# Input projection of a hybrid decoder step on one core: block 0 alone and first, the other blocks in pieces beside the expert gathers

## Chip, cores and metric

One NeuronCore of one Trainium2 chip. The metric is the device time of one execution of the whole program in microseconds (us). All data is float32.

## What is computed

The reference takes 1024 prompt tokens (8 blocks of 128) and 8 sample tokens through one layer of width 1024:

```python
qr, kr, vr, gr, qs, ks, vs = project_in(rms_norm(x, norm1_g), w_in, pos)   # w_in: 1024 x 2816
o_ret, state = retention(qr, kr, vr)          # 4 heads of 128, a state carried from block to block
o_swa = sliding_window_attention(qs, ks, vs)  # 8 query heads, 2 key heads of 64, window 128, sinks
h = x + concat(norm(o_ret) * silu(gr), o_swa) @ w_out
x2 = rms_norm(h, norm2_g)
s = (x2 @ peer_w_q) . sub_keys                # 16 score rows of 128 for each token
idx, gates = two-stage top 16 of each of 8 heads          # 128 experts for each token
y = rms_norm(h + sum_k gelu(peer_u[idx_k] . x2) * gates_k * peer_v[idx_k], final_g)
```

Each token reads 128 rows of the table `peer_uv` (16384 rows of 2048 floats, 8 KB each). Outputs also are the retention state and the key and value windows of prompt and samples. The sample tokens use a given state (2 MB) and given caches of 127 + 1 keys and values.

## The kernel before

**Stages.** First everything is projected, then a loop runs over the 8 blocks.

1. Start-up (`token_transposes`, `project_first`, `key_weights`, the loop over `c` at L528). The 9 token tiles (8 blocks, one tile of 8 sample rows) are normalised, transposed and kept. Eight chunks of `w_in` (352 columns, 1.4 MB) arrive in two buffers; with each, block 0 and the sample rows are projected, and between them `key_weights` multiplies `peer_w_q` by the sub keys (16 steps of two halves) into `keyw`.
2. The rest of the projection (`project_rest`, 56 tiles: 8 chunks of `w_in`, loaded a second time, by 7 blocks). ScalarE copies each tile to a staging buffer (`rest_out`), SyncE stores it to `proj_scratch` (L372). The weights and transposed tokens of this stage lie in `ring`, the home of the gathered rows. Between the tiles the kernel runs the sample rows' attention (`sample`, steps 1 to 8, after tiles 2 to 16) and block 0's `front`: `mixing` (rotation, retention, sliding window) and `picking` (output projection L687, norm, scores L704, the top 16 on VectorE from L1282 on).
3. The expert loop over blocks `b`. GpSimd issues one indirect DMA for each of 128 slots (L452): it brings one 8 KB row for each of 128 tokens (1 MB) into one of 8 rows of `ring`. VectorE makes the dot product (L1431), ScalarE the gelu and a scaled diagonal (`weigh`, L972), TensorE adds the pair of rows to `acc` (`add_pair`, L727) and signals `used`, which lets GpSimd fetch into the rows again. So at most 8 gathers are under way.

**Order of the work.** Every engine runs its own list in order. In the expert loop each engine calls `advance(steps, due, tick)` after each slot: a generator yields the tick (0 to 127, one for each slot) from which its next step of block b+1's `front` may run. The ticks are written by hand: `mixing` at 8 to 41, `picking` from `PICK_AT` = 43, the two halves of the top 16 from `PICK_AT + TOPK_AT` = 77, `HALF_TICKS` = 25 apart. A step that is due waits for its semaphores, and everything behind it on that engine waits too. SyncE issues all plain DMAs in one queue, each behind its wait. The first gather waits for block 0's first half of choices; rows 3 to 7 of the ring and all of TensorE's pairs wait until the last of the 56 tiles is done (L464, L759).

**Homes.** `wo` (32 KB of each partition) holds the sub keys, then the sample rows' caches and state, and only then `w_out`, loaded once (L388). `ring` has 64 KB of each partition.

Of the kernel before, what the change touches and what calls it, by code (L numbers as in the profile page):

```python
# [7 lines left out]
F32 = mybir.dt.float32  # L8
# [38 lines left out]
FIRST = 2 * NCH  # L47
REST = (NB - 1) * NCH
# [10 lines left out]
def step_at(table, tiles):  # L59

    return next((step for step, at in table.items() if at == tiles), 0)


class Steps:


    def __init__(self, eng, sem):
        self.eng, self.sem, self.n, self.base = eng, sem, 0, 0
# [5 lines left out]
    def sync(self):  # L74

        self.eng.wait_ge(self.sem, self.base + self.n)

    def enter(self, turn, per):
        self.first, self.per = self.n, per
        self.base = turn * per  # L80

    def leave(self, turns):
        assert self.n - self.first == self.per, (self.n - self.first, self.per)
        self.base, self.n = 0, self.first + turns * self.per

# [4 lines left out]
def early(q):  # L90

    return 8 + (q - 16) * 11 // 4
# [15 lines left out]
def build(nc, A, out):  # L108
    ctx = ExitStack()
    with ctx:  # L110
# [36 lines left out]

        def heads_of(j):

            return (F[2], F[3]) if j == 0 else (F[1], F[4])  # L150
# [27 lines left out]
        o1 = [0]  # L178

        def part(n):  # L180
            o1[0] += n
            return ring[:, o1[0] - n:o1[0]]

        projs = part(D_IN)
        ropes = part(256)
        sT = part(96)
        ss = part(64)
        sr = part(P)
        pts = part(64)
        osT = part(32)  # L190
        wbuf = [part(KC * CW).rearrange("p (k n) -> p k n", k=KC)]
        early_rows = o1[0] // ROWW
        wbuf.append(part(KC * CW).rearrange("p (k n) -> p k n", k=KC))
        xTrest = part(KC * (NB - 1) * P).rearrange("p (k t) -> p k t", k=KC)
        swp = [h, proj]
        xa = [h[:, :], xlo[:, :]]
        wqT = [work[:, 0:D], work[:, D:2 * D]]
        staging = [(xlo, gfb)[i // 2][:, i % 2 * CW:(i % 2 + 1) * CW] for i in range(STG)]
        mask0 = xlo[:, 2 * CW:2 * CW + 2 * P]


        wof = wo[:].rearrange("p k n -> p (k n)")
        skT = wof[:, 0:NSC]
        xTfirst = wof[:, NSC:NSC + KC * (P + NS)].rearrange("p (k t) -> p k t", k=KC)
        kw = wof[:, 0:NS * P].rearrange("p (s c) -> p s c", s=NS)
        vw = wof[:, D:D + NS * P].rearrange("p (s c) -> p s c", s=NS)
        kwT, sel8 = wof[:, 2 * D:3 * D], wof[:, 3 * D:4 * D]
        st_s = wof[:, 4 * D:8 * D].rearrange("p (s h e) -> p s h e", s=NS, h=RH)

        def token_rows(n):  # L210

            return NS if n == 1 else P

        def tokens_T(n, k):

            if n < 2:
                return xTfirst[:, k, n * P:n * P + token_rows(n)]
            return xTrest[:, k, (n - 2) * P:(n - 1) * P]
# [3 lines left out]
        ld_wq = [sem("ld_wq0"), sem("ld_wq1")]  # L222
        ld_x = [sem("ld_x0"), sem("ld_x1")]
        ld_w = [sem("ld_w0"), sem("ld_w1")]
        ld_wo, ld_gf = sem("ld_wo"), sem("ld_gf")
# [7 lines left out]
        ld_proj, ld_res, ld_mask0 = sem("ld_proj"), sem("ld_res"), sem("ld_mask0")  # L233
# [22 lines left out]
            "rowsx", "roped", "columns", "silu_out", "kv")}  # L256

        proj_d = nc.dram_tensor("proj_scratch", [NTOK, D_IN], F32).ap()
        w_in_v = A["w_in"].rearrange("(k p) n -> p k n", p=P)
# [4 lines left out]
        N_CONST = 8 + NS  # L264
# [8 lines left out]
        def _(sp):  # L273
            def load_x(n):

                if n >= 2:
                    sp.wait_ge(xn_T, n - 1)
                src = x_s if n == 1 else x_p[max(n - 1, 0) * P:max(n, 1) * P, :]
                sp.dma_start(xa[n % 2][0:token_rows(n), :], src).then_inc(ld_x[n % 2], 16)

            def load_w(n):

                if n >= 2:

                    sp.wait_ge(pj_mm, 2 * (n - 1) if n - 2 < NCH else FIRST + (NB - 1) * (n - 1 - NCH))
                c = n % NCH
                sp.dma_start(wbuf[n % 2], w_in_v[:, :, c * CW:(c + 1) * CW]).then_inc(ld_w[n % 2], 16)

            def load_wqT(n):

                if n >= 2:
                    sp.wait_ge(keyw_mm, 2 * n - 2)
                sp.dma_start(wqT[n % 2], A["wqT"][n]).then_inc(ld_wq[n % 2], 16)

            load_x(0)
            for dst, src in [(ident[:], A["c_ident"]), (fold[:], A["c_fold"]), (g1c, A["norm1_g"].rearrange("(k p) -> p k", p=P))]:
                sp.dma_start(dst, src, allow_slow_non_contiguous=True).then_inc(ld_first, 16)
            load_x(1)
            load_w(0)
            load_x(2)  # L300
            load_w(1)
            load_x(3)
            sp.dma_start(skT, A["sub_keysT"]).then_inc(ld_skT, 16)
            load_wqT(0)
            load_wqT(1)
            for c in range(NCH):
                if c + 4 < TILES:
                    load_x(c + 4)
                if 2 * c + 2 < NHC:
                    load_wqT(2 * c + 2)  # L310
                load_w(c + 2)
                if 2 * c + 3 < NHC:
                    load_wqT(2 * c + 3)


            sp.wait_ge(pj_out, FIRST)
            sp.dma_start(proj_d[SEQ:NTOK, C_KS:D_IN], projs[0:NS, C_KS:D_IN]).then_inc(sm["kv"], 16)
            sp.dma_start(ropes[0:NS, :], A["c_rope"][SEQ:NTOK, :]).then_inc(sm["columns"], 16)

            sp.wait_ge(pj_mm, FIRST)  # L320
            sp.wait_ge(keyw_mm, 2 * NHC)
            for s in range(NS):
                sp.dma_start(kw[0:P - 1, s, :], A["cache_swa_k"][s, 1:P].rearrange("w k d -> w (k d)")  # L323
                             ).then_inc(sm["kw"], 16)
            sp.dma_start(st_s.rearrange("p s h e -> p (s h) e"),
                         A["state_ret"].rearrange("s h d e -> d (s h) e")).then_inc(sm["kw"], 16)
            sp.wait_ge(sm["kv"], 16)
            sp.dma_start(kw[P - 1:P, :, :], proj_d[SEQ:NTOK, C_KS:C_VS].rearrange("(a s) c -> a s c", a=1)
                         ).then_inc(sm["kw"], 16)
            for s in range(NS):  # L330
                sp.dma_start(vw[0:P - 1, s, :], A["cache_swa_v"][s, 1:P].rearrange("w k d -> w (k d)")  # L331
                             ).then_inc(sm["vw"], 16)
            sp.dma_start(vw[P - 1:P, :, :], proj_d[SEQ:NTOK, C_VS:D_IN].rearrange("(a s) c -> a s c", a=1)
                         ).then_inc(sm["vw"], 16)
            sp.dma_start(sel8[0:NS, :], A["c_sel8"]).then_inc(sm["vw"], 16)

            sp.wait_ge(xn_T, TILES)
# [7 lines left out]
            for dst, src in loads:  # L345
                sp.dma_start(dst, src, allow_slow_non_contiguous=True).then_inc(ld_const, 16)
# [1253 lines left out]
```

## Time and profile before

| | |
|---|---|
| three runs, us | 3264.59, 3268.72, 3270.58 (median 3268.72) |
| the profiled execution, its own time and its span | 3263.53 us and 3261.7 us |
| busy | TensorE 2315.3 us (71%), VectorE 2024.6 us (62%), ScalarE 1021.3 us (31%), GpSimd 1191.9 us (37%) |
| read from and written to memory | 1143.51 MB and 17.87 MB |
| mean granted TensorE clock | 0.841 |

How to read it: the span runs from the first to the last instruction of the profiled execution; 1.8 us lie around it. Busy times are unions of an engine's instructions. A DMA share is the mean busy share of the core's 16 DMA engines. A clock of 1.00 is 2.4 GHz, 0.50 is 1.2 GHz. A float32 matmul appears as two records, so eight matmuls are "x16".

### The profile page before, as it was taken

The numbers are of one execution on the slowest core, as the hardware profiler recorded it, in microseconds if no ns is written. First come the engines' busy times: TensorE is split into PE (matmuls) and PEld (weight loads), VectorE is DVE, ScalarE is ACT, GpSimd is POOL, SyncE is SP. The second block draws the span as 40 slices with busy tenths as digits, with TensorE's granted clock in tenths as the row PEclk, the third lists the DMA queues.
The fourth block names the chain that finished last, engine by engine and source line by source line (L and its number), as shares of the span: only waits on it lengthen the run. The fifth ranks groups of instructions, "written<-read, shape, count | busy, mean of one in ns | idle before, by whom it ended". The sixth has DMA issues, their size and how long they took to land.

```text
span 3261.7 us, 29956 instructions
## 1 busy us (share of the span) xinstructions
PE 2315.3 (71%) x7730; PEld 863.8 (26%) x7730; DVE 2024.6 (62%) x4947; ACT 1021.3 (31%) x3222; POOL 1191.9 (37%) x1052
## 2 busy tenths in 40 slices
PE   7989996676567656775677567855785678558654
PEld 5556553321122212221222122211221122111111
DVE  2113035658865786579656875687568766875864
ACT  3211101422343234323432334323432343233221
POOL 0000002444444444444444444443444344444442
PEclk9978998897788877887888788878887689789777
DMA  6334215999999999999999999999999999999996
GB/s 221 132 108 138 69 43 210 421 421 408 415 399 422 408 405 409 413 404 406 414 406 395 415 415 410 392 420 409 402 405 410 415 410 421 389 414 422 408 421 279
DMA packets 199565, 1167.67 MB, mean 358 GB/s; under 512 B 23592, under 2 KB 57664, under 8 KB 66272
## 3 DMA queue, kind: packets, MB, share of 16 engines
q0 software_dynamic: 148608, 1082.20, 81.3%
q1 hardware_dynamic: 50784, 83.85, 7.4%
q14 instruction: 147, 1.20, 0.1%
q8 instruction: 26, 0.43, 0.1%
HBM read 1143.51 MB, written 17.87 MB: 356 GB/s over the span
## 4 chain that ended last, share of the span: by engine, by line
DMA 40%; PE 35%; issue 10%; DVE 7%; ACT 5%; SPq 2%; POOL 2%; POOLq 0%; DVEq 0%; ACTq 0%
DMA ring<-in_peer_uv,idxg 38%; PE ps L727 14%; PE ps L496 10%; PE ps L704 7%; DVE ring L1431 3%; POOL ring L452 2%; ACT ring L803 1%; PE ps L478 1%; PE ps L521 1%; DMA out<-work 1%; DVE proj L1289 1%; ACT small L972 1%; PE ps L687 1%; SPq L323 1%; SPq L331 1%
## 5 line engine op out<-in xcount | busy, mean ns | idle before, releaser
L727 PE MATMUL ps<-ring 128*64 128x512 f32 x4096 | 1307.0, 772 | 861.5 <-ACT ring L803 858.0
L452 POOL DMA_INDIRECT ring<-in_peer_uv,idxg x1024 | 1176.0, 1148 | 1495.8 <-PE ps L727 1235.0
L1431 DVE SCALAR_TENSOR_TENSOR ring<-ring,xlo 128x1024 f32<-128x1024 f32 x512 | 626.5, 1224 | 386.3 <-DMA ring<-in_peer_uv,idxg 324.5
L1431 DVE SCALAR_TENSOR_TENSOR ring<-ring,xhi 128x1024 f32<-128x1024 f32 x512 | 626.5, 1224 | 383.2 <-DMA ring<-in_peer_uv,idxg 372.3
L727 PEld LDWEIGHTS ps<-ring 128*64 128x64 f32 x4096 | 300.0, 164 | 1769.0 <-ACT ring L803 1292.8
L972 ACT ACTIVATE small<-small 128x2 f32<-128x2 f32 x512 | 104.1, 203 | 1710.5 <-DVE ring L1431 1710.0
L803 ACT ACTIVATE ring<-gdiag,small 128x64 f32<-128x64 f32 x1024 | 300.3, 340 | 17.7 <-ACT small L972 1.1
L803 ACT ACTIVATE gdiag<-fold,gateg 128x64 f32<-128x64 f32 x1024 | 292.7, 333 | 1.5
L496 PE MATMUL ps<-ring 128*128 128x352 f32 x896 | 278.2, 470 | 7.3 <-ACT xlo L803 6.5
L704 PE MATMUL ps<-keyw,work 128*128 128x512 f32 (+1 forms) x576 | 265.1, 603 | 0.0
L496 PEld LDWEIGHTS ps<-ring 128*128 128x128 f32 x896 | 172.9, 195 | 107.4 <-issue 14.0
L459 POOL COPY idxg<-stage 128x64 uint32<-128x64 uint32 x16 | 7.1, 445 | 526.9 <-DMA stage<-moving 500.1
L704 PEld LDWEIGHTS ps<-keyw,work 128*128 128x128 f32 (+1 forms) x576 | 98.0, 179 | 165.5 <-issue 164.3
L1296 DVE FIND_INDEX8 proj<-proj 128x8 uint32<-128x128 f32 (+3 forms) x432 | 135.0, 328 | 0.0
L1289 DVE MAX8 proj<-proj 128x8 f32<-128x128 f32 (+3 forms) x432 | 109.5, 321 | 37.1 <-ACT proj L803 36.3
L687 PE MATMUL ps<-wo,work 128*128 128x512 f32 x256 | 123.9, 618 | 0.0
L496 PE MATMUL ps<-ring,wo 128*128 128x352 f32 (+1 forms) x256 | 79.4, 464 | 0.0
L972 ACT ACT_TABLE_LOAD x60 | 77.0, 1283 | 1.1
L687 PEld LDWEIGHTS ps<-wo,work 128*128 128x128 f32 x256 | 46.3, 194 | 79.1 <-issue 78.2
L1304 DVE MATCH_REPLACE8 proj<-proj 128x128 f32<-128x128 f32 (+3 forms) x216 | 66.8, 319 | 0.0
L803 ACT ACTIVATE xlo<-ps 128x352 f32<-128x352 f32 x28 | 12.9, 463 | 170.5 <-PE ps L496 143.7
L1068 DVE RECIPROCAL small<-small 128x1 f32<-128x1 f32 (+3 forms) x36 | 5.9, 164 | 86.2 <-ACT small L810 86.2
(191 smaller groups left out, 1527.3 us busy)
## 6 DMA issues: line engine op xcount, KB each, us to landing
ring<-in_w_in SPq DMA_DIRECT2D x16, 1408.0 KB, 6.3
ring<-in_peer_uv,idxg POOLq DMA_INDIRECT x1024
proj<-proj_scratch SPq DMA_DIRECT2D x7, 1408.0 KB
work<-in_wqT SPq DMA_DIRECT2D x16, 512.0 KB, 5.4
h<-in_x_prompt SPq DMA_DIRECT2D x13, 512.0 KB, 5.0
proj_scratch<-xlo SPq DMA_DIRECT2D x28, 176.0 KB, 1.9
proj_scratch<-gfb SPq DMA_DIRECT2D x28, 176.0 KB, 1.8
wo<-in_w_out SPq DMA_DIRECT2D x1, 4096.0 KB, 13.8
```

The lines of the kernel that those rows point to most:

```text
L323: sp.dma_start(kw[0:P - 1, s, :], A["cache_swa_k"][s, 1:P].rearrange("w k d -> w (k d)")).then_inc(sm["kw"], 16)
L452: nc.gpsimd.indirect_dma_start(row[r], None, A["peer_uv"], bass.IndirectOffsetOnAxis(ap=experts, axis=0)).then_inc(ld_row[r], 16)
L496: mm = nc.tensor.matmul(bank[0:token_rows(n), 0:CW], tokens_T(n, k), buf[:, k, :], start=(k == 0), stop=(k == KC - 1))
L687: mm = nc.tensor.matmul(F[2 + n][0:rows, :], lhsT, wo[:, k, n * 512:(n + 1) * 512], start=(k == 0), stop=(k == KC - 1))
L704: mm = nc.tensor.matmul(F[2 + n][0:rows, :], xT[:, k * P:k * P + rows], keyw[:, k, n * 512:(n + 1) * 512], start=(k == 0), stop=(k == KC - 1))
L727: mm = nc.tensor.matmul(acc[side * HP:(side + 1) * HP, n * 512:(n + 1) * 512], row_u[r][:, 0:HP], row_v[r][:, n * 512:(n + 1) * 512], star ...
L803: return nc.scalar.activation(o, i, ACT.Copy, **kw_)
L972: me.did(nc.scalar.activation(gel[:, r:r + 2], dot[:, r:r + 2], ACT.Gelu))
L1289: me.did(nc.vector.max(v16(j)[:, r8 * 8:r8 * 8 + 8], rowsof(j)))
L1296: me.did(nc.vector.max_index(i16(j)[:, r8 * 8:r8 * 8 + 8], v16(j)[:, r8 * 8:r8 * 8 + 8], rowsof(j)))
L1304: me.did(nc.vector.match_replace(rowsof(j), v16(j)[:, 0:8], rowsof(j), TAKEN))
L1431: ins = stt(row_u[r], row_u[r], 1.0, (xlo, xhi)[unit % 2][:], ALU.mult, ALU.mult, accum_out=dot[:, r:r + 1])
```

## The change

Block 0 alone is projected in the start-up, with 8 chunks of 352 columns. All other tiles are projected later in 128 pieces of 176 columns (`PIECES`): block 1 in 16 pieces between block 0's scores and the first pair (`BEFORE`), blocks 2 and 3 in 32 pieces (`EARLY`) beside the first third of block 0's gathers, blocks 4 to 7 and the sample rows in 80 pieces up to tick 32 of block 2. Each group of pieces loads `w_in` again (48 loads of 0.7 MB). Weights, tokens and staging of the pieces lie in `wo`, so `w_out` is loaded anew for each of the first blocks: once to `ring` for block 0, then four times to `wo` (`load_wo`). The transposed tokens of blocks 4 to 7 go to memory (`xT_scratch`) and come back twice. The key weights move behind the start-up, between block 0's `front` steps. The sample rows' attention runs beside the gathers of block 2 (from tick 56 of it, `SAMPLE_AT`). `picking` starts at tick 45 instead of 43. Psum buffers are renumbered: F[4] and F[5] are the pieces'. GpSimd's waits for the projection go. The hardware loops over the blocks are written out.

```diff
+LCH = 16
+LW = D_IN // LCH
+LATE_TILES = [(1,)] * LCH + [(2, 3)] * LCH + [(4, 5, 6, 7, NB)] * LCH
+PIECES = [(l, l % LCH, n) for l, tiles in enumerate(LATE_TILES) for n in tiles]
...
+def late_tick(q):
+
+    if q < EARLY:
+        return 3 + (q - BEFORE) * 9 // 8
+    if q < HALFWAY:
+        return 67 + (q - EARLY) * 97 // 40
+    return TICKS + 59 + (q - HALFWAY) * 101 // 40
...
+            def load_w(c):
+
+                if c >= 2:
+                    sp.wait_ge(pj_mm, c - 1)
+                sp.dma_start(wbuf[c % 2], w_in_v[:, :, c * CW:(c + 1) * CW]).then_inc(ld_w[c % 2], 16)
...
+            def load_late(l):
+
+                if 2 <= l < 2 * LCH:
+                    sp.wait_ge(pj_mm, NCH + (LAST_OF[l - 3] + 1 if l > 2 else 0))
+                elif l >= 2 * LCH and l % (LCH // 2) >= 2:
+                    sp.wait_ge(pj_mm, NCH + LAST_OF[l - 2] + 1)
...
+            def sample():
+                yield SAMPLE_AT
...
+                for s in range(NS):
+                    sp.dma_start(kw[0:P - 1, s, :], A["cache_swa_k"][s, 1:P].rearrange("w k d -> w (k d)")
+                                 ).then_inc(sm["kw"], 16)
...
+            for c in range(NCH):
+                if c + 2 < NCH:
+                    load_w(c + 2)
+                if c + 2 < TILES:
+                    load_x(c + 2)
...
+            move_tokens(0)
+            for q in range(BEFORE):
+                load_late(q + 3)
+                if q == 3:
                     move_picks(0, 0)
...
+                store_late(q)
...
+            for b in range(NB - 1):
+                shift = FIRST_SHIFT if b == 0 else 0
+                if b:
+                    late(b, 6)
+                    store_y(b - 1)
+                late(b, 40 + shift)
+                if b < 4:
+                    load_wo(b + 1)
+                load_residual(b + 1)
+                late(b, 84 + shift)
+                move_tokens(b + 1)
+                late(b, 104 + shift)
+                move_picks(b + 1, 0)
...
-            pool.wait_ge(sm["vb_used"], NS)
-            pool.wait_ge(pj_mm, FIRST + REST - (NB - 1))
...
-                        if unit == early_rows:
-
-                            hold(pool, pj_mm, FIRST + REST)
-
...
+            token_transposes(0)
+            for c in range(NCH):
+                project_first(c)
+                token_transposes(c + 1)
...
+            for tick in range(TICKS):
+                due = advance(steps, due, tick)
+                key_due = advance(keys, key_due, tick)
+            for q in range(BEFORE):
+                project_late(q)
...
+            root(tok_root[0])
+            tokens_in(0)
+            root(tok_root[1])
+            root(tok_root[0])
+            for c in range(NCH):
+                first_out(c)
+                tokens_in(c + 1)
+                if c + 3 < TILES:
+                    root(tok_root[(c + 3) % 2][0:token_rows(c + 3), :])
...
+SAMPLE_AT = 2 * TICKS + 56
+FIRST_SHIFT = 8
+PICK_AT = 45
```

`project_late(q)` is eight matmuls of 128x176 into F[4] or F[5]; it waits for its weights and for the copy of piece q-2. `late_out(q)` (ScalarE) copies piece q to staging and waits for the store of piece q-4. `project_first(c)` waits for its chunk and for the copies of token tile c.

## Rows read from the trace of the kernel before

**Rows 1.** The page: the gathers' DMA queue, and the chain that ended last

```profile
q0 software_dynamic: 148608, 1082.20, 81.3%
DMA 40%; PE 35%; issue 10%; DVE 7%; ACT 5%; SPq 2%; POOL 2%; POOLq 0%; DVEq 0%; ACTq 0%
```

**Rows 2.** Stretches: us, PE, PEld, DVE, ACT, POOL busy, clock, DMA share, GB/s

```profile
280.00:554.00 274.00, 245.36 (x852) 151.95 (x853) 82.04 (x302) 42.99 (x91) 7.88 (x9) 0.96 0.32 114
554.00:3217.00 2663.00, 1809.60 (x5775) 555.93 (x5773) 1873.36 (x4479) 909.48 (x2956) 1180.17 (x1036) 0.82 1.00 409
```

**Rows 3.** Timeline of GpSimd, the first and the ninth gather: start, us, instruction

```profile
501.87 1.10 POOL L452 DMA_INDIRECT ring<-in_peer_uv,idxg  x1 [1.05 <-issue]
...
557.91 1.48 POOL L452 DMA_INDIRECT ring<-in_peer_uv,idxg  x1 [23.48 <-PE ps L727]
```

**Rows 4.** Timeline of TensorE, the first pairs

```profile
553.77 8.81 PE L727 MATMUL ps<-ring 128*64 128x512 f32 x32 [23.54 <-ACT ring L803]
```

**Rows 5.** Groups by line and shape: count, busy us, mean ns

```profile
L727 PE MATMUL ps<-ring 128*64 128x512 f32 x4096 | 1307.0, 772 | 861.5 <-ACT ring L803 858.0 <-issue 2.2
...
L496 PE MATMUL ps<-ring 128*128 128x352 f32 x896 | 278.2, 470 | 7.3 <-ACT xlo L803 6.5 <-issue 0.7
L704 PE MATMUL ps<-keyw,work 128*128 128x512 f32 x512 | 236.0, 604 | 0.0
...
L687 PE MATMUL ps<-wo,work 128*128 128x512 f32 x256 | 123.9, 618 | 0.0
```

**Rows 6.** Timeline of the start-up: projection, key weights, token copies, a square sum

```profile
18.80 5.89 PE L496 MATMUL ps<-ring,wo 128*128 128x352 f32 x16
...
61.47 2.05 PE L521 MATMUL ps<-wo,work 128*128 128x128 f32 x16
...
65.14 4.90 PE L496 MATMUL ps<-ring,wo 128*128 128x352 f32 x16
...
65.34 2.17 ACT L803 ACTIVATE ring<-ps,small 128x128 f32<-128x128 f32 x8 [1.19 <-PE ps L478]
...
70.41 1.23 DVE L1085 SCALAR_TENSOR_TENSOR g2b<-xlo 128x1024 f32<-128x1024 f32 x1 [1.83 <-DMA xlo<-in_x_prompt]
```

**Rows 7.** DMA issues: count, KB each, median us from issue to landing

```profile
ring<-in_w_in SPq DMA_DIRECT2D x16, 1408.0 KB, 6.3
...
h<-in_x_prompt SPq DMA_DIRECT2D x13, 512.0 KB, 5.0
...
wo<-in_w_out SPq DMA_DIRECT2D x1, 4096.0 KB, 13.8
```

**Rows 8.** Packets, MB, share of 16 engines: 295 to 298 us, 214 to 218, 304 to 308

```profile
q1 hardware_dynamic: 1700, 0.87, 101.8%
...
q1 hardware_dynamic: 1056, 1.46, 102.0%
...
q1 hardware_dynamic: 405, 1.66, 101.0%
```

**Rows 9.** DMA of 148 to 152 us, only loads of cached keys

```profile
q1 hardware_dynamic: 171, 0.09, 7.2%
```

**Rows 10.** DMA of 1214 to 1228 us, gathers beside plain transfers

```profile
q0 software_dynamic: 585, 4.26, 73.4%
q1 hardware_dynamic: 446, 1.61, 28.5%
```

**Rows 11.** Timeline of VectorE: block 0's rotation, first and last of its top 16

```profile
278.10 1.43 DVE L1107 TENSOR_TENSOR proj<-work 128x256 f32<-128x256 f32 x4
...
444.47 1.65 DVE L1289 MAX8 proj<-proj 128x8 f32<-128x128 f32 x8 [36.26 <-ACT proj L803]
...
473.42 0.22 DVE L1361 SCALAR_TENSOR_TENSOR proj<-proj 128x64 f32<-128x64 f32 x1
```

**Rows 12.** A stretch in which TensorE waited: columns as in rows 2

```profile
158.00:172.00 14.00, 0.04 (x1) 0.00 (x0) 0.00 (x0) 0.25 (x1) 0.00 (x0) 0.60 0.56 161
```

More of the change, by code:

```diff
@@ new lines, in _ @@
+            steps, keys = front(0), key_weights()
+            due, key_due = next(steps), key_tick(0)
+            for tick in range(TICKS):
+                due = advance(steps, due, tick)
+                key_due = advance(keys, key_due, tick)
+            for q in range(BEFORE):
+                project_late(q)
+            pe.wait_ge(keyw_out, 2 * NHC + 2)
+            pieces, sample_ = late_pieces(), sample()
+            late_due, sample_due = next(pieces), next(sample_)
+            for b in range(NB):
+                if b:
+                    pe.wait_ge(acc_out, b)
+                add_residual(b)
+                steps = front(b + 1) if b < NB - 1 else picking(NB, NS, LAST_AT)
@@ L991, in sum_out @@
                 copy(xT, acc).then_inc(acc_out, 1)
-            steps = front(0)
-            due = next(steps)
-            for q in range(REST):
-                rest_out(q)
-                sample(step_at(SAMPLE_AT, q + 1))
-                due = advance(steps, due, early(q))
-            due = advance(steps, due, TICKS)
-            begin(0)
-            for p in range(EDGE):
-                weigh(0, p)
-            with act.Fori(0, NB - 1) as b:
-                me.enter(b, ACT_STEPS)
-                roots.enter(b, 3)
-                steps = front(b + 1)
+            act.wait_ge(ld_first, 48)
@@ new lines, in _ @@
+            root(tok_root[0])
[7 more added lines that the diff above has]
+                    root(tok_root[(c + 3) % 2][0:token_rows(c + 3), :])
+            steps, keys = front(0), key_weights()
+            due, key_due = next(steps), key_tick(0)
+            topk = PICK_AT + TOPK_AT
+            for tick in range(topk + HALF_TICKS):
+                due = advance(steps, due, tick)
+                key_due = advance(keys, key_due, tick)
@@ L1007, in _ @@
+            for q in range(BEFORE):
+                late_out(q)
+            steps_0, due_0 = steps, due
+            pieces, sample_ = late_pieces(), sample()
+            late_due, sample_due = next(pieces), next(sample_)
+            for b in range(NB):
+                begin(b)
+                if b:
+                    sum_out(b - 1)
+                steps = front(b + 1) if b < NB - 1 else picking(NB, NS, LAST_AT)
                 due = next(steps)
-                for p in range(EDGE, PAIRS):
+                for p in range(PAIRS):
+                    tick = 2 * p + 1
@@ L1463, in _ @@
+            due = next(steps)
+            topk = PICK_AT + TOPK_AT
+            steps_0, due_0 = steps, advance(steps, due, topk + HALF_TICKS - 1)
+            sample_ = sample()
+            sample_due = next(sample_)
+            for b in range(NB):
+                take_over(b)
+                steps = front(b + 1, wmask[:]) if b < NB - 1 else picking(NB, NS, LAST_AT)
                 due = next(steps)
-                for unit in range(2 * EDGE, SLOTS):
+                for unit in range(SLOTS):
```

1029 lines of the change are left out of this document (517 added, 512 removed).

## The prediction

> **What bounds the kernel now.** I read the stretches first. From 554 us to 3217 us the 16 DMA engines are busy all the time (share 1.00), while TensorE is busy 1810 of 2663 us [rows 2]. Ahead of that, from 280 to 554 us, their share is 0.32. The queue table says who fills them: the gathers take 81.3% of 16 engines' span, 2652 us, and in the chain DMA has the largest share, 40% [rows 1]. So from 554 us on every byte that is added costs its DMA time, and idle TensorE or ScalarE time there is worth nothing. The other bound is the start-up: the first gather is issued at 501.87 us, the ninth at 557.91 us [rows 3], because the pairs begin at 553.77 us [rows 4]. The change trades one against the other. It brings the pairs forward, and it moves transfers from a stretch with idle DMA engines into one without. Two sums decide: when do the pairs begin, and what do the moved and added transfers cost.
>
> **Start-up, block 0 alone.** One would think that eight projections of 4.9 us and a few transposes [rows 6] take 60 us. The queues say otherwise. SyncE issues chunk c+2 and behind it token tile c+2, and the chunk waits for projection c. ScalarE does the root of tile c+2 ahead of the copies of tile c+1, without which projection c+1 can't start. So a period holds, one after the other: chunk and tile landing, 6.3 us and 1.4 us behind it (a tile's 128 packets of 4096 B at 160 ns over 16 engines, and as much again for contention) = 7.7; square sum 1.23 and three short operations, 2.0; the copy of the chunk, 0.5; the token copies 2.17; the projection 4.9 [rows 6 to 8]. That is 17.3 us. The first projection ends at about 18 us (before, it began at 18.80 with the same loads under way [rows 6]), six periods follow, and a last one without a load, 9 us. TensorE works 6 of 17 us; where it waited like that the granted clock was 0.60, so partly 1.2 GHz [rows 12]. At 1.2 GHz the period would be 22 us; I take 19.5. End of projection 7: 18 + 117 + 10 = 145 us, rotation done at 151. Bounds: 131 and 160.
>
> **Block 0's front with the key weights.** Before, it ran from the rotation at 278 us to the top 16 at 444 us [rows 11], 166 us, filled by projection tiles of 278.2/56 = 5.0 us [rows 5]. Now 32 halves of key weights at 1.02 us [rows 6] stand between. Retention and sliding window are a ping-pong of engines, estimated at 42 us with 16 halves in their gaps; then the output projection 123.9/8 = 15.5 us at the mean clock, 13.7 at full clock; norm and transposes beside 8 halves, 14; two score groups of 236.0/32 = 7.4 us, at full clock 6.85, with 8 halves of 1.2 us put between them, 23 [rows 5]; one copy, 1. Sum 94 us, and 5 for a lower clock: the top 16 starts at 250 us. It takes 29.0 us [rows 11] and 1.5 for the end, the move and the first gather 3.8: first gather at 284 us. Bounds of this part: 76 us (TensorE's own work) to 120.
>
> **The sixteen pieces of block 1** stand ahead of the first pair. Seven are done while the top 16 runs; for the others SyncE issues the weights only behind `move_picks`, so they compete with the first 8 gathers. A piece is 4.9/2 = 2.4 us of TensorE. Its weights are 1024 packets, 64 for each engine. In the gather stretch plain packets and gather packets pass about one for one (446 to 585 in 14 us) [rows 10]. So a load lasts up to 64 x (36 + 320) ns = 22.8 us while gathers are queued, and 2.3 us when they have run dry. (320 ns is 2652 us x 16 over some 132,000 rows of 8 KB [rows 1].) I take 23 us for the first, then 7 x 3.5: pairs begin 48 us after the first gather, at **332 us**, 222 us sooner than at 554. Bounds 296 and 357.
>
> **What the gather stretch gets.** Prices by packet from [rows 8]: 512 B 48.9 us / 1700 = 28.7 ns, 1408 B 61.8 ns, 4096 B 159.6 ns; 704 B lies between, 35.8 ns. After the pairs begin:
> - 29 loads of 176 columns (l = 19 to 47): 29 x 1024 x 35.8 / 16 = 66.5 us
> - 96 stores of full tiles: 96 x 128 x 35.8 / 16 = 27.5 us (the samples' 16 are nothing)
> - `w_out` four times: 4 x 1024 x 159.6 / 16 = 40.9 us
> - kept tokens twice, 4.3 MB at 415 GB/s: 10.3 us
> - sample rows: state in 5.1, out 4096 x 28.7 / 16 = 7.3, window stores 3.7 us
> - the 16 loads of cached keys and values. Here I priced by the row, not by bytes: in 4 us 171 packets at 7.2% of 16 engines, so one engine alone at 23.4 ns each [rows 9]. 16 x 127 x 23.4 = 47.5 us on one engine that every gather needs too. Cost 47.5, at least 3 if it were spread.
>
> Sum 209 us; 165 if the last were free. Nothing in the old gather stretch goes away. Writing out the loops takes nothing off either, as the DMA engines had no gap there.
>
> **Waits.** TensorE, ScalarE and SyncE now wait for transfers inside the loop, with `add_pair` and `weigh` queued behind. Eight gathers in flight cover 8 x 2.56 = 20.5 us. (1) Ticks 3 to 38 of block 0: 32 pieces 75 us, 18 pairs at 1307.0/512 = 2.55 [rows 5], 46 us, and mixing about 20 = 141 us of TensorE; DMA 36 x 2.56 + 16 x 2.3 + 9 = 138. Both full; and ScalarE waits for stores that stand behind weight loads. I take 20 us. (2) `w_out` asked for some 8 ticks (21 us) ahead of its use in blocks 1 and 2, landing in 13.8 us alone [rows 7] and 64 x 0.48 = 31 us beside gathers; tokens and weights at tick 67 likewise: mostly covered, 5 us together. (3) The samples' two waits for the one engine, 10 us beyond its work; block 1's columns behind weight loads, 5. Sum **40 us**, bounds 0 and 100. The pieces' 112 x 2.4 = 269 us of TensorE and 112 short ScalarE copies cost nothing else: the gather stretch has 853 us without TensorE work. Without that cover, as in (1), they are the bound. `picking` two ticks later is hidden by the ring. GpSimd issues the same 1024 gathers.
>
> **Sum.** 3263.5 (the profiled execution) - 222 + 209 + 40 = 3290.5 us. The median of the three runs is 5 us above that execution, so **3296 us**, slower by 0.8%.
>
> **Rivals.**
> - *A, faster: the start is early and the waits stay covered.* The gathers' queue would not hold up weight loads. Mechanism: plain packets of 704 B pass several to one gather packet. With 5 at a time a load lasts 2.3 + 13 x 0.32 = 6.5 us, the nine pieces go 17 us sooner, waits (1) and (2) shrink by 25; with the period at 17.3 us, another 19. 3296 - 61 = 3235. For it: the plain packets of [rows 10] have 3.6 KB in the mean, and none of 704 B is shown. It decides from a pair start of about 300 us. The Trainium skill, "DMA: Bandwidth & Descriptors", section "Queues, rings and completion order", says that an engine takes whole packets of typically 9 to 17 descriptors from one queue before it turns to the next; by that rule the load would be as short as here and the sum 3235, by the row it is 3296; the trace does not agree, as the one for one of [rows 10] speaks against it. Chance 0.28.
> - *B, much slower: loads late in the loop become the bound.* A load of 22.8 us has a lead of three weight steps, about 20 us. If each of 29 then stops the pairs by 3 us more than the ring covers, it is 3296 + 29 x 3 = 3383. Against it: when the pairs stop, the gathers run dry and a load takes 2.3 us. Chance 0.15.
> - *C, a draw.* The start-up gain equals the transfers, both by accident: 3268. Chance 0.08.
> - *D, the change does not bring the gathers forward.* If front and keys kept the old 166 us instead of 99, the pairs would start at 399 and the time be 3363. It ends where B does and shares B's chance.
>
> My forecast, slower by 10 to 90 us, has 0.49. The bounds of its terms (-36 and +25 on the start, -44 on the one engine, -40 and +60 on the waits) don't fall together; with A and part of B the range is 3228 to 3365. A measurement here tells 0.2%, 6.5 us, from nothing. Faster 0.28, same 0.08, slower 0.64.
>
> **What would show it.** Right: projection periods of 17 to 22 us in the start-up with ScalarE idle before its roots; first gather near 284 us, pairs near 332; DMA share near 1 from there, with the plain queue's time up by about 209 us; 16 cache loads in block 2 at 22 GB/s or with the pairs stopped; blocks 3 to 7 as before. Wrong: a period near 9 us, weight loads that land in 6 us beside gathers, or DMA gaps of more than 100 us in blocks 0 to 2.

## The result, and the profile after

| | before | after |
|---|---|---|
| median of the runs, us | 3268.44 (3264.59 to 3270.58, 4 runs) | 3322.77 (3316.09 to 3326.58, 4 runs) |
| the profiled execution, its time and its span | 3263.5, 3261.7 | 3324.5, 3322.7 |
| first gather, first pair, us | 501.9, 553.8 | 270.8, 321.9 |
| from the first pair to the end of the span, us | 2707.9 | 3000.8 |

The ratio is 1.0172, 95% interval [1.0159, 1.0184]: the changed kernel is 1.7% slower. The forecast was 3296 us, 0.8% slower; the sign and the range held, but the loss is twice what I said, 54 us and not 27.

The timelines of GpSimd and of TensorE of the changed kernel (start, us, instruction, in brackets the idle time before it and who ended it) show the first, the ninth gather and the first pair, 231 to 233 us sooner than in [rows 3, 4]:

```profile
270.84 1.10 POOL L554 DMA_INDIRECT ring<-in_peer_uv,idxg  x1 [0.97 <-POOL idxg L563]
...
324.56 0.94 POOL L554 DMA_INDIRECT ring<-in_peer_uv,idxg  x1 [43.21 <-PE ps L847]
```

```profile
321.86 3.65 PE L847 MATMUL ps<-ring 128*64 128x512 f32 x16 [1.71 <-ACT ring L918]
```

So the start gained 232 us, and the rest of the program lost 293. The stretches from the first pair on (columns as in rows 2: length, the busy time of five engines, clock, DMA share, GB/s), beside the one of 1.00 in [rows 2]:

```profile
322.00:1000.00 678.00, 528.40 (x2433) 299.26 (x2432) 353.12 (x786) 209.04 (x681) 220.16 (x202) 0.88 0.94 367
1000.00:1800.00 800.00, 535.46 (x2198) 236.91 (x2196) 488.43 (x1191) 248.10 (x789) 284.90 (x256) 0.82 0.91 361
1800.00:3280.00 1480.00, 1005.15 (x3145) 298.46 (x3147) 1061.88 (x2599) 493.49 (x1626) 655.30 (x581) 0.83 1.01 414
```

The last is as full as before. The first two lack 6% of 678 and 9% of 800 us, 113 us of DMA time. The queue table over 322 to 3280 us of the changed kernel (packets, MB, share of 16 engines), and over 554 to 3217 us of the kernel before:

```profile
q0 software_dynamic: 146594, 1067.58, 88.6%
q1 hardware_dynamic: 66911, 80.33, 7.8%
```

```profile
q0 software_dynamic: 146527, 1067.13, 98.1%
q1 hardware_dynamic: 7808, 21.28, 2.2%
```

The plain queue q1 took 7.8% of 2958 us = 231 us, before 2.2% of 2663 = 59: 172 us more. The gathers (q0) took 2621 and 2612, 8 us more. Those two and the gaps, 111 us more by the same rows (100% less the shares: 3.4% of 2958 against -0.4% of 2663), make 291 of the 293 us. The gaps are what is left over, so the sum closes by itself, and each share is rounded to 0.1%, 3 us. The account has three lines: start -232, transfers +180, gaps +111. My forecast had -222, +165 and +85 (44.5 for the one-engine loads, 40 for waits).

Where the gaps are, the waits tell. The view of waits of the changed kernel (engine, line, waited for: us, times, longest), those behind the start-up for transfers other than gathers:

```profile
ACT wo L918 <- DMA proj_scratch<-wo: 100.1, 12, 17.2
DVE work L1216 <- DMA qsT<-in_c_rope: 35.8, 1, 35.8
...
PE ps L578 <- DMA wo<-proj_scratch: 32.1, 1, 32.1
PE ps L805 <- DMA wo<-in_w_out: 31.7, 2, 26.1
DVE work L1216 <- DMA out<-work: 28.8, 4, 20.0
PE ps L686 <- DMA wo<-proj_scratch: 23.9, 1, 23.9
...
PE ps L620 <- DMA wo<-in_w_in: 19.2, 3, 12.5
```

L918 is ScalarE's copy of a piece, which waits until its staging buffer is stored; L1216 the rotation, of block 1 for its columns (35.8 us) and of later blocks until `y` of an earlier block is stored (28.8 us in four waits); L578 and L686 the transposes of the samples' cached keys and the product with their values; L805 `w_out`; L620 the pieces' weights.

The stretches with the large gaps (columns as in rows 2):

```profile
322.00:490.00 168.00, 139.56 (x743) 103.28 (x742) 70.57 (x145) 53.86 (x168) 38.44 (x38) 0.89 0.88 317
580.00:620.00 40.00, 29.37 (x130) 17.72 (x131) 12.74 (x22) 9.57 (x31) 12.27 (x10) 0.82 0.77 294
960.00:1000.00 40.00, 35.98 (x155) 20.61 (x156) 12.33 (x20) 11.19 (x38) 11.88 (x11) 0.88 0.77 296
1195.00:1225.00 30.00, 10.34 (x48) 5.92 (x49) 12.92 (x27) 5.26 (x18) 4.60 (x3) 0.66 0.62 238
1340.00:1540.00 200.00, 103.21 (x404) 36.91 (x402) 106.74 (x292) 49.65 (x156) 56.82 (x54) 0.74 0.79 298
1720.00:1760.00 40.00, 11.35 (x30) 3.76 (x32) 11.10 (x18) 6.33 (x25) 5.84 (x6) 0.66 0.77 311
```

Their gaps are 20 us (the 32 pieces at the start of block 0), 9 and 9 (the first weights of a group), 11 (the rotation that waits for `y`), 42 (the sample rows) and 9 (`w_out` for block 3), 100 of the 113.

### The profile page after: what moved, and what is told of

It reads as the page before. It is cut to its first block, busy times and chain, and to the rows that moved or that the text cites. A ratio compares the mean times of both kernels' runs of the same rounds, so it can differ in the third digit from the quotient of the medians.

```text
span 3322.7 us, 29034 instructions
## 1 busy us (share of the span) xinstructions
PE 2297.2 (69%) x8754; PEld 990.1 (30%) x8754; DVE 2022.9 (61%) x4947; ACT 1028.5 (31%) x3291; POOL 1171.3 (35%) x1052
## 4 chain that ended last, share of the span: by engine, by line
DMA 36%; PE 33%; DVE 11%; issue 6%; SPq 5%; ACT 4%; POOL 3%; another core or an unknown queue 2%; POOLq 0%; DVEq 0%; ACTq 0%
DMA ring<-in_peer_uv,idxg 24%; PE ps L847 13%; PE ps L824 6%; PE ps L620 6%; DVE ring L1538 5%; DMA proj_scratch<-wo 4%; SPq L390 3%; POOL ring L554 3%; DMA wo<-in_w_out 2%; SPq L385 2%; PE ps L601 2%; PE ps L805 2%; ACT ring L918 2%; DMA wo<-in_w_in 2%
## 5 line engine op out<-in xcount | busy, mean ns | idle before, releaser
L554 POOL DMA_INDIRECT ring<-in_peer_uv,idxg x1024 | 1158.0, 1131 | 1834.0 <-PE ps L847 1591.9
L847 PE MATMUL ps<-ring 128*64 128x512 f32 x4096 | 1236.1, 736 | 701.5 <-ACT ring L918 700.8
L847 PEld LDWEIGHTS ps<-ring 128*64 128x64 f32 x4096 | 290.8, 158 | 1490.8 <-ACT ring L918 1016.9
L620 PE MATMUL ps<-wo 128*128 128x176 f32 (+1 forms) x2048 | 351.4, 330 | 87.9 <-issue 68.8
L620 PEld LDWEIGHTS ps<-wo 128*128 128x128 f32 (+1 forms) x2048 | 310.1, 188 | 174.4 <-issue 140.7
L918 ACT ACTIVATE ring<-gdiag,small 128x64 f32<-128x64 f32 x1024 | 300.3, 340 | 16.8
L918 ACT ACTIVATE gdiag<-fold,gateg 128x64 f32<-128x64 f32 x1024 | 292.7, 333 | 1.5
L918 ACT ACTIVATE wo<-ps 128x176 f32<-128x176 f32 (+3 forms) x135 | 41.7, 311 | 449.8 <-PE ps L620 278.7
L805 PE MATMUL ps<-wo,work 128*128 128x512 f32 x224 | 110.9, 629 | 31.7 <-DMA wo<-in_w_out 31.7
L601 PE MATMUL ps<-ring,wo 128*128 128x352 f32 x128 | 56.3, 611 | 69.6 <-ACT ring L918 35.2
L805 PEld LDWEIGHTS ps<-wo,work 128*128 128x128 f32 x224 | 40.2, 195 | 103.9 <-issue 103.9
L1216 DVE TENSOR_TENSOR work<-proj,qsT 128x256 f32<-128x256 f32 x64 | 22.8, 418 | 64.6 <-DMA qsT<-in_c_rope 35.8
## 6 DMA issues: line engine op xcount, KB each, us to landing
wo<-in_w_out SPq DMA_DIRECT2D x4, 4096.0 KB, 33.2
```

Of the source, the lines that this page charges most:

```text
L554: nc.gpsimd.indirect_dma_start(row[r], None, A["peer_uv"], bass.IndirectOffsetOnAxis(ap=experts, axis=0)).then_inc(ld_row[r], 16)
L601: mm = nc.tensor.matmul(F[c % BANKS][:, 0:CW], tokens_T(0, k), wbuf[c % 2][:, k, :], start=(k == 0), stop=(k == KC - 1))
L620: mm = nc.tensor.matmul(F[4 + q % 2][0:token_rows(n), 0:LW], late_T(n, k), buf[:, k, :], start=(k == 0), stop=(k == KC - 1))
L805: mm = nc.tensor.matmul(F[2 + n][0:rows, :], lhsT, weights[:, k, n * 512:(n + 1) * 512], start=(k == 0), stop=(k == KC - 1))
L847: mm = nc.tensor.matmul(acc[side * HP:(side + 1) * HP, n * 512:(n + 1) * 512], row_u[r][:, 0:HP], row_v[r][:, n * 512:(n + 1) * 512], star ...
L918: return nc.scalar.activation(o, i, ACT.Copy, **kw_)
```

## Experiments

Two theories stood against each other for the gaps. **One engine:** the samples' 16 cache loads lie on one DMA engine that all gathers need. **The queue:** SyncE has one plain queue, and what is late in it (stores behind 0.7 MB loads, first weights behind kept tokens) stops ScalarE or TensorE for longer than eight gathers last. Beside them, two prices were to be tested: of the start-up period, and of a load beside gathers. Gains below are differences of the ratios to the kernel before on the same chip, times 3265 us; each ratio has an interval of about ±0.0016, 5 us, so a gain is good to 7 us or so (to 10 where the kernel with three edits is in it). Where stretches or issue times of two kernels are compared, it is one profiled execution of each.

### The cache loads cut in two, after and before

```diff
-sp.dma_start(kw[0:P - 1, s, :], A["cache_swa_k"][s, 1:P]...).then_inc(sm["kw"], 16)
+for lo, hi in ((0, 112), (112, P - 1)):
+    sp.dma_start(kw[lo:hi, s, :], A["cache_swa_k"][s, 1 + lo:1 + hi]...).then_inc(sm["kw"], 16)
```

The same for `vw`; the waits count 2 * NS + 1 transfers.

> The kernel after the change with each of the 16 loads of cached keys and values cut in two, 112 and 15 partitions, so that no load lies on one DMA engine. One-engine theory: what the one engine takes is lost whole, 47.5 us less 3 for the spread work, and the waits of TensorE for the keys (32 us) and of VectorE and TensorE for the values shrink with it: 3268 to 3280 us, 45 to 55 us below the changed kernel, and the stretch of block 2 in which the DMA share fell is full. Rival, the queue of SyncE: the samples' rows wait behind other transfers whatever engine they lie on, and the work would come in 0 to 15 us faster only: 3308 to 3323 us.

Measured: 3275.24 us, ratio 1.0032 [1.0015, 1.0048], against 1.0172: 46 us. The one-engine theory holds. SyncE's timeline and the stretches of the changed kernel show how it stood still:

```profile
1344.53 56.71 SPq L385 DMA_DIRECT2D wo<-in_cache_swa_k  x7
...
1404.27 105.52 SPq L390 DMA_DIRECT2D wo<-in_cache_swa_v  x8
```

```profile
1375.00:1395.00 20.00, 0.41 (x7) 0.32 (x6) 6.04 (x10) 0.25 (x1) 2.50 (x2) 0.60 0.53 204
```

In these 20 us TensorE works 0.4 us, because the transposes of the keys stand in its list ahead of the next pair. In the second half of them the gathers have run dry, and what moves is 22 GB/s, the rate of one engine as in [rows 9]. SyncE too is held: issuing 15 loads takes 162 us. Where nothing else moves it is 3 us each (two in 5.93 us from 1395.31 us), which is one load on one engine (127 packets at 23.4 ns are 2.97 us). With the loads cut, the same stretch of that kernel is full:

```profile
1375.00:1395.00 20.00, 18.24 (x77) 7.73 (x77) 7.87 (x14) 9.46 (x25) 8.34 (x8) 0.99 1.05 375
```

The Trainium skill, "DMA: Bandwidth & Descriptors", section "Why a DMA increments its semaphore by 16 and not by 1", says that a transfer runs on the largest number of engines, up to 16, that divides its outermost dimensions, so that 127 partitions put everything on one. The trace agrees: 22 GB/s with 127, a full stretch with 112 (and 15).

The control does the same in the kernel before:

> The kernel before with the same 16 loads cut into 112 and 15 partitions. There they lie in the start-up beside projections: both theories expect little, 0 to 8 us less than 3268.4. If it gained as much as the changed kernel does, the cut itself and not the place in the loop would be what matters.

Measured: 3240.92 us, ratio 0.9932 [0.9915, 0.9948]: 22 us gained, where I expected 0 to 8. The 16 loads lie in the start-up there, and I had thought them hidden behind projections. They weren't: over 100 to 200 us TensorE is busy 81 us before and 98.6 with the cut. These two lines are of the kernel before and of the one with the cut:

```profile
100.00:200.00 100.00, 81.05 (x365) 54.49 (x363) 5.54 (x14) 16.70 (x34) 0.00 (x0) 0.85 0.33 106
```

```profile
100.00:200.00 100.00, 98.58 (x457) 66.44 (x456) 5.54 (x14) 20.09 (x43) 0.00 (x0) 0.95 0.45 142
```

The first gather comes 27 us sooner with the cut (474.87 and not 501.87 us). So of the 46 us that the loads cost in the changed kernel, 22 were being paid already; moving them into the loop doubled their cost.

### The token tile ahead of the chunk

```diff
 for c in range(NCH):
+    if c + 2 < TILES:
+        load_x(c + 2)
     if c + 2 < NCH:
         load_w(c + 2)
-    if c + 2 < TILES:
-        load_x(c + 2)
```

> The kernel after the change with the token tile c+2 issued ahead of weight chunk c+2 on SyncE, nothing else. Theory (the forecast's account of the period): the tile waits only for the transposes of tile c, so landing, square sum, root and copies run beside the projection, and the period falls from 17 to 19 us to 9 or 10; the first gather and the first pair come about 50 us sooner (from 271 and 322 us to about 220 and 272) and the time falls by as much, to about 3273 us. Rival 1: TensorE's lower clock or the weight chunk itself holds the period (14 us or more): 3300 us or above. Rival 2: the start comes 50 us sooner but the loop gives a part back, as the transfers of blocks 0 to 2 are the same: a gain clearly below the shift of the first pair.

Measured: 3279.76 us, ratio 1.0048 [1.0031, 1.0064]: 40 us, where 50 were expected. A period of the changed kernel, from its timeline:

```profile
68.56 6.60 PE L601 MATMUL ps<-ring,wo 128*128 128x352 f32 x16 [10.66 <-ACT wo L918]
...
75.19 0.40 SPq L327 DMA_DIRECT2D ring<-in_w_in  x1
75.64 0.57 SPq L321 DMA_DIRECT2D xhi<-in_x_prompt  x1
82.44 1.22 DVE L1203 SCALAR_TENSOR_TENSOR keyw<-xhi 128x1024 f32<-128x1024 f32 x1 [15.45 <-DMA xhi<-in_x_prompt]
...
83.89 0.20 ACT L925 ACTIVATE small<-small 128x1 f32<-128x1 f32 x1 [15.47 <-DVE small L1180]
...
84.34 2.16 ACT L918 ACTIVATE ring<-ps,small 128x128 f32<-128x128 f32 x8
86.65 2.10 PE L601 MATMUL ps<-ring,wo 128*128 128x352 f32 x3 [10.62 <-ACT ring L918]
```

It is the ring of the forecast: chunk and tile are issued, the tile lands 6.8 us later, square sum, root, copies, projection. With the tile first, the timeline of that kernel:

```profile
43.81 6.66 PE L601 MATMUL ps<-ring,wo 128*128 128x352 f32 x16 [2.36 <-ACT wo L918]
...
58.05 6.83 PE L601 MATMUL ps<-ring,wo 128*128 128x352 f32 x16 [6.70 <-ACT ring L918]
...
68.11 6.66 PE L601 MATMUL ps<-ring,wo 128*128 128x352 f32 x16 [2.36 <-ACT ring L918]
```

The period is 9.9 to 14.2 us, 11.3 in the mean of seven, where I had expected 9 or 10. The first gather is at 226.9 us, 44 sooner, and the first pair at 275.5, 46 sooner; that arrives in the time, as far as 7 us can be told. One reason for the rest is the projection, which takes 6.7 us and not 4.9 [rows 6]: see the last section.

### The stores on a queue of their own

```diff
+def put_late(q):
+    _, c, n = PIECES[q]
+    act.wait_ge(pj_out, NCH + q + 1)
+    act.dma_start(proj_d[...], late_stage(q)[...]).then_inc(st_pj[q % STG], 16)
 ...
                 yield late_tick(q) + 2
                 late_out(q)
+                yield late_tick(q) + 3
+                put_late(q)
```

SyncE's `store_late` is empty in turn, its waits with it.

> The kernel after the change with the stores of the small pieces issued by ScalarE, on a DMA queue of its own, a tick behind each copy; SyncE no longer waits for the pieces' copies. Queue theory: the 100 us that ScalarE waits for stores which stand behind weight loads, and the waits of SyncE's loads behind stores, make 25 of the excess of idle DMA time: 3298 to 3313 us, ScalarE's wait for the stores under 30 us. Rival: those waits are covered by the eight gathers in flight, and the time stays within 5 us of 3322.8; or ScalarE, which now issues and waits for its own copies, loses a few us (up to 3335).

Measured: 3301.57 us, ratio 1.0121 [1.0104, 1.0138]: 17 us by the ratios, 21 by the medians. ScalarE's wait for stores, 100.1 us, is gone from the waits, and the time lies in the range that the queue theory had (3298 to 3313). But only a part of the gain is what the theory meant. At the end of block 0's 32 pieces the gap shrinks by 6 us (over 440 to 580 us the DMA share is 1.00 where it was 0.96). Another 9 us is the stretch from 1720 to 1760, long behind the last piece: its share is 1.01 and not 0.77, and TensorE's wait of 26 us for `w_out` is gone, because the samples' state, for whose store `w_out` has to wait, was stored in 56 us and not in 81. Why that store was faster here is not shown. SyncE is relieved too: in the changed kernel, beside the first gathers, issuing one store held it for many us:

```profile
272.51 7.15 SPq L351 DMA_DIRECT2D proj_scratch<-wo  x1
...
282.07 13.69 SPq L351 DMA_DIRECT2D proj_scratch<-wo  x1
```

### The first weights of a group asked for earlier

```diff
-        return 67 + (q - EARLY) * 97 // 40
-    return TICKS + 59 + (q - HALFWAY) * 101 // 40
+        return 75 + (q - EARLY) * 87 // 40
+    return TICKS + 67 + (q - HALFWAY) * 91 // 40
 ...
-                    yield late_tick(FIRST_OF[l0]) - 4
+                    yield late_tick(FIRST_OF[l0]) - 12
```

> The kernel after the change with the pieces of blocks 2 to 7 due 8 ticks (about 20 us) later, at tick 75 instead of 67 and packed a little closer, while their first loads are asked for at the same tick as now. Lead theory: TensorE's two waits of 22 us for the first weights (at 590 and 964 us) go, and with them 5 to 10 us of idle DMA each: 3303 to 3313 us. Rival: the eight gathers in flight (20.5 us) cover those waits already and closer packing costs elsewhere: within 5 us of 3322.8.

Measured: 3313.75 us, ratio 1.0153 [1.0136, 1.0170]: 6 us, and the interval reaches that of the changed kernel. Alone it decides nothing. The two gaps close (DMA share 1.02 and 0.98 where it was 0.77), at 590 us, where TensorE waited 22 us,

```profile
590.63 4.32 PE L620 MATMUL ps<-wo 128*128 128x176 f32 x16 [22.37 <-issue]
```

and at 964 us, where it waited 21.6. But the lead is lost again: gather 80 (of 0 to 1023) is issued 16 us sooner than in the changed kernel, gather 112 is 3 us later. The pieces stand closer, and ScalarE waits 127.1 us for stores and not 100.1; that this is the reason is argued and not shown. On top of the other edits this one was worth more (next part).

### All together

> The kernel after the change with three edits together: the loads of cached keys and values cut in two, the token tile issued ahead of the chunk, the pieces' stores on ScalarE's own queue. If the three causes are separate, their gains of 47.5, 43 and 21 us add: 3211 us. If the waits of one hide behind another, less: 3225 to 3240. Both would beat the kernel before.

> As the three edits together, with the later pieces of the lead kernel as well: a further 10 to 20 us, 3191 to 3201 us, if the lead theory holds; the same as the three edits together within 5 us if it does not.

Measured: the three edits 3213.36 us, ratio 0.9856 [0.9830, 0.9881]; with the later pieces 3190.09 us, 0.9776 [0.9760, 0.9792]. Against the changed kernel the three give 3.16% or 103 us, where 46 + 40 + 17 = 103: within the noise, three separate causes that add. The fourth adds 26 us, give or take 10, which is more than the 6 it had alone; against the 10 to 20 that I expected it can't be told apart. With the stores out of the way the lead that it gains at gather 80 is kept (17 us there, 13 at gather 128). The kernel that results is 2.2% faster than the one before the change. Its stretches from the first pair on:

```profile
278.00:950.00 672.00, 545.42 (x2500) 299.14 (x2497) 372.30 (x853) 215.16 (x701) 227.91 (x211) 0.90 0.97 384
950.00:1750.00 800.00, 597.53 (x2336) 254.92 (x2336) 535.14 (x1306) 270.83 (x861) 317.94 (x280) 0.82 0.99 397
```

The gaps are 3% and 1%, 28 us where they were 113. What is left stands mostly at the start of block 0 (share 0.90 over 278 to 446 us) and at the rotation that waits for `y` (0.66 over 1105 to 1140).

### What a load beside gathers costs

Added to the kernel before, in SyncE's loop over blocks, five in each turn; by the trace they were issued beside the gathers of blocks 1 to 6 (891 to 2622 us). In the second kernel without the wait and each copy to its own place:

```diff
+def one_more():
+    if extra[0]:
+        sp.wait_ge(ld_spare, 16 * extra[0])
+    extra[0] += 1
+    sp.dma_start(spare, A["w_in"].rearrange("(k p) n -> p k n", p=P)[:, :, 0:176]).then_inc(ld_spare, 16)
```

> The kernel before, SyncE's loop over blocks written out, with 30 copies of 176 columns of w_in (1024 packets of 704 B each) into a scratch in DRAM spread over blocks 3 to 7 and the gathers beside them; nobody but SyncE waits for one. Price theory: the gather stretch has no gap, so each costs its packets' time, 30 x 1024 x 35.6 ns / 16 = 68 us: 3333 us, give or take 10. Rival: small packets slip in between the gathers' packets and cost less than half of that: under 3300 us. If it comes to clearly more than 80 us, loads cost the loop more than their own time even where no engine waits for them.

> As the kernel before with added copies, of which that run's trace shows 25 (25 x 1024 packets; the 30 in its expectation was a miscount), but each goes to a place of its own and SyncE never waits for one. There 76 us were added, where the packets' time is 25 x 1024 x 36.9 ns / 16 = 59 us. If the other 17 us came from SyncE's waits for a copy (27 us each beside gathers), which hold its y stores and block loads, they go: 3265 + 59 = 3324 us. If they stay, 3341, a copy costs the gathers more than its packets' time.

Measured: 3341.24 us, ratio 1.0235 [1.0218, 1.0252], and 3335.32 us, ratio 1.0220 [1.0203, 1.0237]. So 25 copies cost 77 us, and 72 without SyncE's waits, 2.9 us each in the mean. The packets account for less; the pages' lines for the plain queue, first of the kernel before, then of the second kernel:

```profile
q1 hardware_dynamic: 50784, 83.85, 7.4%
```

```profile
q1 hardware_dynamic: 76784, 101.87, 9.0%
```

26,000 packets more took 9.0% of 3333 less 7.4% of 3262 = 59 us, 36 ns each as estimated in the forecast, 2.3 us for a load. SyncE's waits were not the cause of the excess, as the second kernel keeps 13 of 18 us.

The trace of the second kernel shows where the time went, and it isn't spread over the copies. The rotation of a later block, on VectorE, waits five times for the store of `y`, about 15 us each. The line of its waits, and then from its timeline one of the five, with the copy, the store and the rotation:

```profile
DVE work L1112 <- DMA out<-work: 74.2, 5, 15.2
```

```profile
1920.45 0.59 SPq L421 DMA_DIRECT2D spare_scratch<-in_w_in  x1
1935.94 0.35 SPq L408 DMA_DIRECT2D out<-work  x1
...
1960.51 1.43 DVE L1112 TENSOR_TENSOR work<-proj,qsT 128x256 f32<-128x256 f32 x4 [14.86 <-DMA out<-work]
```

A copy stands in the plain queue ahead of the store; in the kernel before VectorE has no such wait. VectorE's dot products stand behind the rotation in its list, so the pairs stop and GpSimd waits 20 to 22 us for one. The same 35 us of a block in the second kernel and in the kernel before:

```profile
1940.00:1975.00 35.00, 11.96 (x38) 3.36 (x40) 14.30 (x32) 6.05 (x22) 7.96 (x8) 0.56 0.70 274
```

```profile
1905.00:1940.00 35.00, 21.46 (x95) 9.47 (x93) 22.39 (x45) 9.93 (x36) 15.57 (x14) 0.85 1.01 408
```

That is a gap of 10 us, five times. The issue times of the gathers agree: against the kernel before they fall behind by 10 to 13 us between ticks 12 and 36 of blocks 2 to 6, 58 us of 71 in all, and by 3 us in the mean over the rest of a block with its four other copies, whose packets take 9. So a copy for which nothing waits cost less than its packets' time, under 1 us (the gathers' own packets took 78.8% of 3333 against 81.3% of 3262, 25 us less), and one that holds up an awaited store cost over 11. That the total lies near the sum of the packets is in part luck.

The changed kernel has this wait too. Here the store of block 1's `y` was issued 1 us behind a weight load:

```profile
1188.15 0.38 SPq L345 DMA_DIRECT2D wo<-in_w_in  x1
...
1189.20 1.96 SPq L453 DMA_DIRECT2D out<-work  x1
...
1211.18 1.43 DVE L1216 TENSOR_TENSOR work<-proj,qsT 128x256 f32<-128x256 f32 x4 [19.95 <-DMA out<-work]
```

It is the gap of 11 us from 1195 to 1225. None of the four edits moves it: with all of them the rotation still waits 19.7 us. No run issues this store ahead of the load, so what it would give back is not measured.

### Leaving the loads out

```diff
+n_k = KC if l < LCH + 3 else 1
-sp.dma_start(buf, w_in_v[:, :, c * LW:(c + 1) * LW]).then_inc(landed, 16)
+sp.dma_start(buf[:, 0:n_k, :], w_in_v[:, 0:n_k, c * LW:(c + 1) * LW]).then_inc(landed, 16)
```

> The kernel after the change, where each of the 29 weight loads of small pieces from l = 19 on brings one of its eight row groups (128 packets of 704 B instead of 1024): the pieces are computed with older weights, so left out are 7/8 of those loads. Their packets' time is 29 x 896 x 35.6 ns / 16 = 57.8 us: 3265 us if only their transfer costs. Wait theory: stores and first loads no longer stand behind them in the queue, so the 20 to 30 us of waits that the stores' own queue and the later pieces took away go too: 3235 to 3248 us.

> The kernel with the four edits together (3190 us), with the same 7/8 of the 29 loads left out. If the four edits took away nearly all waits for those loads, what is left is the price of their packets, 57.8 us: 3132 us, give or take 8. If much more goes, waits for the loads were still there; if much less, the gathers' packets did not pay the full price of the loads.

Measured: in the changed kernel 3242.15 us, ratio 0.9938 [0.9916, 0.9960], 76 us less, 18 more than the packets' 58. Waits fit that rest (TensorE's longest for first weights is 9.1 us where it was 22.4), but no run measures them apart. With the four edits 3146.02 us, ratio 0.9635 [0.9615, 0.9654], 46 us less, under the 50 to 66 I expected. There the gathers don't get the whole of what is set free. That blocks 0 to 2 are nearly TensorE-bound (81% busy from 278 to 950 us) is a reason for it which is argued and not shown. So the same 29 loads are worth 46 or 76 us, by what stands behind them.

For `w_out`, with the second to fourth load cut to one row group (`wo[:, 0:n_k, :]`, n_k = 1 for b > 1):

> The kernel with the four edits together, where the second to fourth reload of w_out bring one of eight row groups (the output projections of blocks 2 on are computed with partly old contents): 3 x 896 x 172 ns / 16 = 28.9 us less if only the packets cost, 3161 us; 3140 to 3150 if waits for w_out (the trace shows two, 8 to 26 us) cost the loop as much again.

Measured: 3164.10 us, ratio 0.9699 [0.9679, 0.9720], 25 us less: the price of the packets (28.9) within the noise, with no sign of waits behind it once the other edits are in.

## Why the forecast was right in its sign and wrong in its size

**What bounds it, and the trade.** Right. From the first pair on the DMA share of the changed kernel is 0.97, the start came forward and the transfers filled the loop, as forecast.

**Start-up: 222 us forecast, 232 measured.** The period of 19.5 us was 18.7 in the mean of five (from 31.44 to 124.93 us), the end of projection 7 came at 142 instead of 145. The front took less: the top 16 began at 235.4 instead of 250, the first gather at 270.8 instead of 284. The 48 us from there to the pairs were 51. That some 22 us of this gain come from the cache loads having left the start-up (by the control) I had not counted.

**Transfers: 165 forecast (without the one engine), 180 measured.** The packets' times hold: 36 ns for 704 B. The plain queue took 172 us more; the gathers' own records 8 more, which I had not counted. That every packet costs the loop its own time, the premise of this sum, is borne out by the run without most of `w_out`; the added copies cost less than that where nothing waited for them.

**One-engine loads: 44.5 + 10 of waits forecast, 46 measured (42 by the gap).** Right in mechanism and size. But their old place was not free, as the control showed.

**Waits: here the step failed.** It is term (2), "mostly covered, 5 us together", and with it the cover of 20.5 us by eight gathers.

- Terms (1) and (3), without the samples, were 20 us for the pieces at the start of block 0 and 5 us for block 1's columns. Both lie in the stretch from 322 to 490 us, whose gap is 20 us. That fits.
- The first weights of the two later groups left gaps of 9 and 9 us, behind waits of TensorE of 22.4 and 21.6 us. I let the ring cover a lead of four ticks, 10 us, for 2 MB of tokens and a load that itself takes over 20 us beside gathers.
- `w_out` for block 3 left 9 us. SyncE asked for it at 1721.46 us and not some 8 ticks ahead of its use, because it first waited 81 us for the store of the samples' new state (2 MB), which leaves the same buffer. TensorE then waited 26 us.
- The store of block 1's `y` behind a weight load left 11 us. It stands in no term.

So term (2) came to 27 us instead of 5, and a wait of the same kind that I had not listed to 11. Against that the first terms were 5 lower and the samples' gap 12 lower (42, where 44.5 + 10 were forecast), and 13 us of gaps lie spread over other stretches. That makes some 28 us more gap than forecast. The start (-10) and the transfers (+15) leave 5, and the median lies 2 us below the profiled execution where I had put it 5 above (-7): 26, the miss of 27.

The sentence that the pieces' 112 ScalarE copies "cost nothing else" is not settled. The stores on a queue of their own gave 17 us, but of the gaps that went with them about half lie beside pieces and the other half in the wait for `w_out`. The sign of being wrong that I had named, gaps of more than 100 us in blocks 0 to 2, was reached or nearly so: 113 us up to 1800 us, of which 9 are block 3's. "Blocks 3 to 7 as before" failed by the same 9 us.

**Rival A** said that small packets pass the gathers several at a time, so that a load lands in 6.5 us. It is refuted. The queue table of the changed kernel from 286 to 296 us, while the first gathers and a weight load are in flight:

```profile
q0 software_dynamic: 514, 3.77, 91.3%
q1 hardware_dynamic: 513, 0.36, 11.1%
```

That is one for one. An added copy landed in 27.1 us (median of 13) beside gathers, `w_out` in 33.2 us where I had 31. What I made of the packets of 9 to 17 descriptors in this rival was not sound: equal counts over 10 us would also come from an engine that takes several records of each queue in turn, so they neither contradict this nor does a short load follow from it. **Rival B** (29 late loads that stop the pairs by 3 us each, 87 us) had the mechanism that was missing in my sum, at less than half its size: 38 us of gaps in four places, and not 3 us at each load. **C** and **D** did not occur.

## What to carry to other kernels

When work is moved into a stretch where one resource is full, price the transfers by packet, and then go through every wait, the old ones too, with the question of what now stands ahead of the awaited transfer in its queue: `y`'s store was no wait before, and behind a 0.7 MB load it stopped the pairs for 20 us and more. The number of gathers in flight covers one such wait only if nothing else is late in the same 20 us. A transfer thought hidden should be tested where it is: the cache loads cost 22 us in the kernel before, where they looked free.

## What the runs showed of the hardware that I had not expected

- After waits in the start-up the projection began at 1.2 GHz. Stretches of the changed kernel, the first and the second half of a projection that began after 10.6 us of idle TensorE:

```profile
86.70:90.00 3.30, 3.30 (x6) 2.06 (x7) 0.00 (x0) 0.00 (x0) 0.00 (x0) 0.50 0.02 5
90.00:94.40 4.40, 4.40 (x13) 2.61 (x13) 0.00 (x0) 0.00 (x0) 0.00 (x0) 0.74 0.00 0
```

The granted clock is 0.50 in the first, 1.2 GHz, and a projection took 6.4 to 7.8 us where an undisturbed one took 4.90 [rows 6]. Even after the idle 2.36 us of the kernel with the tile first it took 6.66 us; the granted clock was 0.65 in its first 3.2 us there.
- Issuing is not always short: beside gathers one store held SyncE for 13.7 us, and eight loads that lie on one engine for 105 us, most of it beside gathers.
- A load of 0.7 MB beside gathers for which nothing waited cost the loop under 1 us of time, less than the 2.3 us that its packets took; behind it, a store that was waited for cost over 11.
- Gather and plain packets of very different size, 8 KB and 704 B, still pass one for one (514 to 513 in 10 us).
